# Two-block transformer kernel: block one's expert tokens gathered per expert, with the selection's 32 columns as the stationary operand

## The reference, cut to what matters

```python
def _hier_moe(h, w_rg, b_rg, w_re, b_re, w_gate, w_up, w_down):      # block one
    # h = rms(x) * ffn_norm_g, 256 tokens x 1024
    # best of 4 groups by g_logits; in that group the best 2 of 8 experts
    combine = ...                                   # 256 x 4 x 8, two weights a token, else 0
    for g in range(N_GROUPS):
        a = einsum('td,edf->tef', t, w_gate[g])     # 1024 -> 256
        b = einsum('td,edf->tef', t, w_up[g])
        m = silu(a) * b * combine[:, g, :, None]
        y = y + einsum('tef,efd->td', m, w_down[g]) # 256 -> 1024
```

## Time and profile before

| | |
|---|---|
| median of 3 executions | 914.57 us (913.44 to 915.78) |
| profiled execution | 915.7 us, its span 913.8 us |
| mean granted TensorE clock | 0.992 |
| busy: PE, weight loads, DVE, ACT | 856.8, 552.4, 505.8, 348.6 us |
| DMA moved | 285.35 MB, mean 312 GB/s |
| block one: routing from, first gate/up, last gate/up | 288.6, 312.4, 514.1 us |
| block two: first gate/up, last gate/up | 676.8, 891.3 us |

### The profile page before, as it was taken

The page is one execution under the profiler, slowest core; times in us unless marked ns, Lnnn a source line. Parts: engine busy times, 40 slices in busy tenths (PEclk is TensorE's granted clock), DMA queues, the critical chain, the costliest instruction groups (busy, mean ns, idle before and its releaser), DMA issues.

```text
span 913.8 us, 14985 instructions
## 1 busy us (share of the span) xinstructions
PE 856.8 (94%) x5584; PEld 552.4 (60%) x5584; DVE 505.8 (55%) x1119; ACT 348.6 (38%) x686; POOL 22.3 (2%) x41
## 2 busy tenths in 40 slices
PE   8999999999999998998888899999899999999995
PEld 6778557987977533443333379876664555455552
DVE  5877668555456666433333486789764643333335
ACT  5674435455355322222222366754621111111113
POOL 1010111000000000000000000000000000000000
PEclk9999999999999999999999999999999999999998
DMA  9655894556626899999999997530769899999991
GB/s 356 253 196 223 320 382 190 184 184 232 257 112 258 330 409 362 427 426 425 426 426 425 422 370 294 215 155 1 292 231 369 338 406 423 425 425 425 425 418 55
DMA packets 29958, 285.35 MB, mean 312 GB/s; under 512 B 3113, under 2 KB 5577, under 8 KB 8913
## 3 DMA queue, kind: packets, MB, share of 16 engines
q1 hardware_dynamic: 26400, 278.25, 75.2%
q0 software_dynamic: 1136, 3.74, 1.3%
q10 hardware_dynamic: 2368, 2.64, 0.9%
HBM read 283.56 MB, written 1.06 MB: 311 GB/s over the span
## 4 chain that ended last, share of the span: by engine, by line
PE 65%; DMA 17%; DVE 11%; ACT 4%; issue 2%; SPq 1%; DVEq 0%; ACTq 0%
DMA ring<-in_experts 13%; PE bank L1162 11%; PE bank L743 8%; PE bank L1182 7%; PE bank L745 7%; PE bank L744 7%; PE bank L1210 5%; PE bank L1167 3%; DMA arena<-in_mem 2%; DVE ring_r L526 2%; PE bank L1174 2%; PE bank L1118 2%; DMA ring<-in_ada 1%; PE bank L720 1%; PE bank L1264 1%
## 5 line engine op out<-in xcount | busy, mean ns | idle before, releaser
L526 DVE TENSOR_TENSOR ring_r<-ring,ring_r 128x1024 fp32r<-128x1024 f32 (+1 forms) x84 | 99.4, 1212 | 65.9 <-ACT ring_r L519 65.7
L1162 PE MATMUL bank<-ring,arena 128*64 128x256 f32 x992 | 113.9, 382 | 1.0 <-DVE arena L2498 0.6
L519 ACT ACTIVATE ring_r<-ring 128x1024 fp32r<-128x1024 f32 (+1 forms) x84 | 85.0, 1046 | 68.1 <-PE bank L745 67.4
L743 PE MATMUL bank<-HT_r,ring_r 128*128 128x256 f32 x352 | 102.0, 290 | 1.3 <-DVE arena_r L2066 0.7
L745 PE MATMUL bank<-HT_r,ring_r 128*128 128x256 f32 x352 | 99.6, 283 | 0.0
L1182 PE MATMUL bank<-ring,arena 128*64 128x512 f32 (+1 forms) x488 | 91.7, 604 | 0.7 <-DVE arena L2575 0.7
L1162 PEld LDWEIGHTS bank<-ring,arena 128*64 128x64 f32 x992 | 69.8, 137 | 36.5 <-issue 6.4
L1777 ACT ACTIVATE arena<-bank 128x512 f32<-128x512 f32 (+1 forms) x64 | 31.4, 490 | 137.8 <-PE bank L1162 80.3
L744 PE MATMUL bank<-XN_r,ring_r 128*128 128x256 f32 x288 | 81.5, 283 | 0.0
L1167 PE MATMUL bank<-ring,arena 128*32 128x512 f32 x480 | 57.7, 597 | 22.5 <-DMA ring<-in_experts 22.0
L1210 PE MATMUL bank<-arena_r 64*128 64x512 f32 x496 | 74.1, 417 | 4.3 <-DVE arena_r L2555 3.8
(11 more groups left out here) (503 smaller groups left out, 1422.3 us busy)
## 6 DMA issues: line engine op xcount, KB each, us to landing
ring<-in_experts SPq DMA_DIRECT2D x61, 2048.0 KB, 15.3
ring<-in_experts SPq DMA_DIRECT2D x61, 1024.0 KB, 12.6
ring<-in_ada SPq DMA_DIRECT2D x12, 2048.0 KB, 11.4
ring<-in_win SPq DMA_DIRECT2D x5, 2048.0 KB, 15.1
ring<-in_hy SPq DMA_DIRECT2D x3, 2048.0 KB, 18.1
ring<-in_mk SPq DMA_DIRECT2D x2, 2048.0 KB, 11.0
ring<-in_mv SPq DMA_DIRECT2D x2, 2048.0 KB, 9.5
ring<-in_wo SPq DMA_DIRECT2D x2, 2048.0 KB, 8.7
```

The costliest lines, as they stand in the source:

```text
L519: nc.scalar.activation(R(h), w, ACT.Copy).then_inc(sem("w_high"), 1)
L526: nc.vector.tensor_tensor(R(w), w, R(h), ALU.subtract).then_inc(sem("w_low"), 1)
L743: mm(ps, R(ah), R(bh), start=first, stop=False)
L1162: last = mm(gu_bank[g * wide:(g + 1) * wide, 0:256], xw[:, k, :], w[k // 4][:, k % 4, g * 256:(g + 1) * 256], start=k == 0, stop=k == KD - 1)
```

## The change

The 32 gather matmuls for all 512 positions go. Each expert's window is gathered on its own, in four stages: DVE copies the 32 columns of the selection (`picked`); PE uses them as stationary operand and XN, in fp32, as moving one, for two blocks of tokens and two halves of the channels, each product in a column group of its own (`token_rows`: four matmuls of 512 columns, output 32 pairs x 512 channels each); ACT copies the bank to SBUF (`rows_sb`); PE turns it (`rows_T`: four transposes); DVE adds the two blocks of tokens and scales with the gains into `xwin` (`scaled_tokens`). The split of the tokens in high and low goes in block one, and so do the idle products in the loop. Gather of expert e+2 stands in step e behind `to_tokens`, ahead of down of e-1; the turn of e+1 stands behind `gu_T` of e-1. The first expert's window is compared directly, without the full selection, and what DVE did ahead of the gather for the weights, the ranks and the lists now comes behind the first window.

XN is kept whole for this, so the weights beside the ring move: expert 4's gate/up half to the arena's columns 4096 to 8191, expert 5's to 0 to 4095, its down half to HT. Expert 4's is issued before experts 2 and 3, as soon as the cross attention's last product is done; expert 5's behind expert 3. The bias product of block two moves ahead of the counting products, and POOL loads its operands earlier.

```diff
+        + ([("bias", 1, (5,)), ("cnt1", 1, (0,)), ("cns1", 1, (7,)), ("sct1", 4, (1, 2, 3, 4)), ("slots1", 1, (7,))] if one else
+           [("sct2", 4, (0, 1, 2, 3)), ("cnt2", 1, (6,)), ("cns2", 1, (7,)), ("gx2", 8, (4, 5, 6, 7, 4, 5, 6, 7)), ("slots2", 1, (5,))])
...
+        sorted_at, picked = three(area(at + 3584, TT * (NPAIR + WIN[1])), TT), area(8704, 128).rearrange("p (i t w) -> p i t w", i=2, t=TT)
+        rows_sb = area(8192, 512)
...
-        by_tile = three(area(KD * SORTED + NPAIR, 4096), 4)
-        outside = (((three(XNf[:, :], 4), three(HTf[:, :], 4)), ROW[:, :]),
-                   ((by_tile[:, :, 0:512], by_tile[:, :, 512:1024]), X[:, :, :].rearrange("p t d -> p (t d)")),
+        outside = (((three(area(4096, 2048), 4), three(area(6144, 2048), 4)), ROW[:, :]),
+                   ((three(area(0, 2048), 4), three(area(2048, 2048), 4)), HTf[:, :]),
...
+                for e in range(RING):
+                    if b == 0 and e == 2:
+                        filled(f"xv{XH - 1}")
+                        for q in range(2):
+                            beside_ring(0, q)
+                    in_ring(e)
...
-                    sp.wait_ge(sem("xn_low"), TT)
+                    for q in range(2):
+                        beside_ring(1, q)
                     filled("rt1")
-                    for q in range(2):
-                        beside_ring(0, q)
-                    filled("cns1")
                     sp.dma_start(outside[1][1], w[RING + 1, :, GU:SLOT]).then_inc(sem("outside1"), 16)
-                    for q in range(2):
-                        filled("gx1", 4 * q + 3)
-                        beside_ring(1, q)
...
+                if b == 1:
+                    pe.wait_ge(sem("onehot"), 32)
+                    pe.wait_ge(sem("mask_row"), 1)
+                    ps = take(pe, "bias")
+                    full(mm(ps[0:H1, :], relb[0:BUCKETS + 1, :], oneh[0:BUCKETS + 1, :], start=True, stop=True), "bias")
+                occupy(f"cnt{b}", 0, b)
...
+                def token_rows(i):
+                    for h in range(2):
+                        for t in range(TT):
+                            g = wide * (2 * h + t)
+                            last = mm(list_bank[g:g + wide, :], picked[:, i, t, :], XN[:, t, h * 512:(h + 1) * 512], start=True, stop=True)
+                    return last
+                def rows_T():
+                    for c in range(4):
+                        last = tr(list_bank[:, c * P:(c + 1) * P], rows_sb[:, c * P:(c + 1) * P], ident)
+                    return last
+                def gather_rows(e, i):
+                    pe.wait_ge(sem("picked"), e + 1)
+                    pe.wait_ge(sem("xwin1"), e * 2)
+                    token_rows(i).then_inc(sem("gathered"), 1)
+                def gather_T(e):
+                    pe.wait_ge(sem("rows_sb"), e + 1)
+                    rows_T().then_inc(sem("rows_T"), 1)
...
+                        if b == 1 and not (isinstance(e, int) and e == last_step):
+                            gather_T(e + 1)
+                    first_window = isinstance(e, int) and e == 0
+                    if b == 1:
+                        pe.wait_ge(sem("xwin1"), e * 2 + 2)
+                    elif not first_window:
+                        pe.wait_ge(sem("xwin2"), e)
+                    gate_up(xsT[:, :, 0:wide] if first_window and b == 2 else xwin[:, r % 2], gate_arrived(e, r)).then_inc(sem(f"gu_done{b}"), 1)
+                    if first_window:
                         if b == 1:
-                            for _ in range(1 if isinstance(e, int) and e < unrolled else 3):
-                                mm(list_bank[:, 0:256], ident, T("iota")[:, 0:256], start=True, stop=True)
-                    first_window = isinstance(e, int) and e == 0
-                    if not first_window:
-                        pe.wait_ge(sem(f"xwin{b}"), e)
-                    gate_up(xsT[:, :, 0:wide] if first_window else xwin[:, r % 2], gate_arrived(e, r)).then_inc(sem(f"gu_done{b}"), 1)
-                    if first_window:
+                            gather_rows(1, 1)
+                            gather_T(1)
                         beside_first()
                     if 0 not in first:
                         pe.wait_ge(sem(f"y_low{b}"), e - 1)
                         to_tokens(r % 2).then_inc(sem(f"to_tokens{b}"), 1)
+                    if b == 1 and not (isinstance(e, int) and e + 2 > last_step):
+                        gather_rows(e + 2, r % 2)
                     if isinstance(e, int) and e == last_step:
...
+                if b == 1:
+                    ready(pe, "cnt1")
+                    pe.wait_ge(sem("picked"), 1)
+                    token_rows(0).then_inc(sem("gathered"), 1)
+                    gather_T(0)
+                    ready(pe, "rT1", 1)
...
+            def rows_out(e):
+                act.wait_ge(sem("gathered"), e + 1)
+                A_(rows_sb, expert_banks(1)[3][:, :], ACT.Copy).then_inc(sem("rows_sb"), 1)
...
+                        if e == 0:
+                            rows_out(1)
+                        rows_out(e + 2)
...
+                def scaled_tokens(e, i):
+                    x = expert_tiles(1)[4][:, i]
+                    V.reduce_sum(x, expert_banks(1)[3][:, :].rearrange("p (k t w) -> p k w t", k=KD, t=TT), AXX).then_inc(sem("xwin1"), 1)
+                    dve.wait_ge(sem("xwin1"), e * 2 + 1)
+                    by_half = x.rearrange("p (c h) w -> p c h w", h=2)
+                    gains = C("ffn_norm_g", 0, KD).rearrange("p (h c) -> p c h", h=2)
+                    return V.tensor_tensor(by_half, by_half, gains.unsqueeze(3).broadcast_to([P, 4, 2, WIN[1]]), ALU.mult)
+                def tokens_in(e, i):
+                    dve.wait_ge(sem("rows_T"), e + 1)
+                    if not (isinstance(e, int) and e < 2):
+                        dve.wait_ge(sem("gu_done1"), e - 1)
+                    scaled_tokens(e, i).then_inc(sem("xwin1"), 1)
+                def pick(e, i):
+                    s = window(e, i)
+                    V.tensor_copy(picked[:, i], sorted_at[:, :, bass.ds(s, WIN[1])]).then_inc(sem("picked"), 1)
...
+                    places(picked[:, 0, 0, :], WIN[1], 0)
+                    link(places(picked[:, 0, 1, :], WIN[1], 1))
+                    second_places(picked[:, 0, 0, :], WIN[1], 0)
+                    second_places(picked[:, 0, 1, :], WIN[1], 1).then_inc(sem("picked"), 1)
+                    places(sorted_at[:, 0, 0:NPAIR], NPAIR, 0)
+                    link(places(sorted_at[:, 1, 0:NPAIR], NPAIR, 1))
+                    second_places(sorted_at[:, 0, 0:NPAIR], NPAIR, 0)
+                    second_places(sorted_at[:, 1, 0:NPAIR], NPAIR, 1)
+                    tokens_in(0, 0)
+                    V.memset(sorted_at[:, :, NPAIR:NPAIR + WIN[1]], 0.0).then_inc(sem("pad"), 1)
...
+                if b == 1:
+                    dve.wait_ge(sem("pad"), 2)
+                    pick(1, 1)
                 free(of_tokens(ps), f"cns{b}")
                 ready(dve, f"cns{b}")
                 link(V.reduce_sum(rank4, prod4.rearrange("p k t e -> p (k t) e"), AXX))
+                if b == 1:
+                    weights()
...
+                if b == 1:
+                    tokens_in(1, 1)
+                    pick(2, 0)
+                    pick(3, 1)
...
                 def x_window(e, i):
+                    if b == 1:
+                        tokens_in(e, i)
+                        if not (isinstance(e, int) and e + 2 >= NE):
+                            pick(e + 2, i)
+                        return
                     s = window(e, i)
                     dve.wait_ge(sem(f"gu_done{b}"), e - 1)
```

More of the change, by code:

```diff
@@ L599, in experts, with in_ring @@
                     sp.dma_start(outside[0][1], w[RING, :, GU:SLOT]).then_inc(sem("outside0"), 16)
-                for e in range(RING):
+                first = 3 * RING
+                ways = 2 - b
+                def in_ring(e):
                     load(base + e, w[e, :, 0:GU], GU)
@@ L1141, in beside_first @@
                     full(slot_lists(b, ps), f"slots{b}")
-                    if b == 1:
-                        pe.wait_ge(sem("onehot"), 32)
-                        pe.wait_ge(sem("mask_row"), 1)
-                        ps = take(pe, "bias")
-                        full(mm(ps[0:H1, :], relb[0:BUCKETS + 1, :], oneh[0:BUCKETS + 1, :], start=True, stop=True), "bias")
                 gu_bank, guT_bank, d_bank, list_bank = expert_banks(b)
@@ L1750, in moe @@
                 A_(gex, cand4, ACT.Exp).then_inc(sem("logit_exp"), 1)
-                for k in (0, 1, 2, 3, 4, 6) if b == 1 else range(0, KD, 2):
-                    ps = got(act, f"gx{b}", k)
-                    if shift is None:
-                        last = A_(xsT[:, k, 0:NPAIR], ps[:, :], ACT.Copy, scale=gain(k))
-                    else:
```

(29 more changed lines are left out.)

140 lines of the change are left out of this document (70 added, 70 removed).

## The result

The changed kernel takes 921.31 us (median of 6 runs, 918.88 to 922.94), the one before 914.38 beside it (6 runs, 913.29 to 917.65). The ratio is 1.0063 with a 95% interval of 1.0043 to 1.0082: 5.8 us by the ratio, 6.9 by the medians. Measured a second time it was 923.19 for 914.44, ratio 1.0089 (1.0069 to 1.0108). Forecast were 922.9 and +8.3.

The account below looks back on a forecast made before the run. Bound: bytes moved from 361 us on, so only DMA idle before expert 10's down half counts. Down 6 ends 8.0 us later (0.5, 5.8, 1.8 rounded), plus 0.3 behind it: +8.3, 922.9 us from 914.57; range 917.5 to 926.

Parts of the forecast that it names:

- What sets the time: Block one: expert 6's down product frees the slot for expert 10's down half; DMA idles until that issue, 8.0 us later.
- Earlier loads: Expert 4's gate/up half loaded in the idle stretch before the ring: 4.9 us of transfer moved, worth 0 us.
- The prologue: From the positions to block one's first gate/up product: gather matmuls removed, that product starts at 307.4, 4.9 us earlier.
- The first step takes it back: Gathers and token waits between expert 0's gate/up and down products make down 0 end 0.5 us later.
- Longer steps: Six steps from down 0 to down 6 each gain gather and turn, lose an idle product: +0.97 each, +5.8 us.
- The stalls: Steps 5 to 7: PE waits for DVE's y_low, then for tokens ahead of the gather; 4.9 us together, +1.8.
- Behind it: After expert 10's down half is issued: the next step takes 7.1 us instead of 6.6, adding 0.3 us.
- Rival A: The 4.9 us earlier first gate/up product carries through and added step work is hidden: 909.7 to 913.7 us; chance 0.11.
- Rival B: The gather costs less than its form and DVE pieces vanish in longer steps: about 0, 914.6 us; chance 0.05.
- Rival C: PE's clock falls in prologue without idle products; one or two steps add 6 to 12 us: 929 to 935; chance 0.05.

Follow-up runs that it names:

- b_fill3: Kernel before with three idle products instead of one in each of the first eight expert steps of block one; 916.49 us, ratio 1.0023.
- b_late: Kernel before with DVE's four pieces of the extra windows moved from steps 4 to 7 to steps 25 to 28; 911.01 us, ratio 0.9956.
- a_late: Changed kernel with DVE's four pieces of the extra windows moved to steps 25 to 28; 916.47 us, ratio 1.0021.
- b_late_fill0: Kernel before with DVE's extra-window pieces in steps 25 to 28 and no idle product in the first eight steps; 910.71 us, ratio 0.9956.
- a_loads: Changed kernel with expert 4's gate/up half issued behind expert 3's again, undoing the early load; 923.55 us, ratio 1.0097; on a second occasion 920.98, 1.0077.
- a_again: Changed kernel run once more, unaltered; 923.19 us, ratio 1.0089.
- a_all: Changed kernel with DVE's extra-window pieces in steps 25 to 28, gather behind the down product, idle products in the last step; 916.82 us, ratio 1.0022.
- a_idle: Changed kernel with idle products in its waits: around the first two turns and three in the last expert step; 920.05 us, ratio 1.0059.
- b_last0: Kernel before without the three idle products in block one's last expert step; 916.02 us, ratio 1.0013.
- a_down: Changed kernel with the gather of expert e+2 behind the down product of e-1, ACT's copies reordered to match; 922.97 us, ratio 1.0084.

## Why the prediction was right, and where its sizes were off

- **What sets the time.** Right: the issue of expert 10's down half. b_fill3, b_late and a_late moved it by +2.65, -3.3 and -3.5 us, and block two's first gate/up product went by +2.0, -2.5 and -3.4 (the times by +2.1, -4.0 and -3.8 by the ratios, in which the clock has a part). b_late_fill0 shows the bound of the rule: next to no gain once the engines never idle.
- **Earlier loads, 0.** Right by a_loads: the issue doesn't move.
- **The prologue, 4.9 us earlier.** Right: 4.88 relative. On before's clock the first product starts at 307.48 for the 307.4 forecast.
- **The first step takes it back, +0.5.** Nearly: -0.1. Its chain came nearly as forecast (gate/up 1 at 316.0 on before's clock for 316.35); the down product started 0.86 behind the gather ahead of it, where the forecast had 1.1, and DVE stood idle for 0.31 to 0.33 ahead of most picks, where the forecast had 0.52 for the register load.
- **Longer steps, +5.8.** +5.3: a step grew by 0.88 for 0.97, since a gather takes 0.86 to 0.88 before the next product starts.
- **The stalls, +1.8.** +0.7, the largest miss ahead of the issue. The two waits came in the order forecast, but the second was 1.10 for 1.25, step 5 had 0.32 for 0.6, and the first was 0.51 and 0.76 for 0.75 and 1.0.
- **Behind it, +0.3.** Wrong in sign: -1.2 up to 428 us, of which the faster start of the stream is about 1. Then +1.2 came back by block two, and the clock's fall in the tail, which the sum had at nothing, is 1.5 us by itself. So the sum of +8.3 became +5.9 at block two and +5.8 by the ratio.
- **Where luck helps.** The medians are 6.9 apart, the second time 8.7, and in a_again's profile the issue is 8.2 later than before, close to the forecast 8.0. That closeness isn't the sum's merit: 2.3 of the 8.2 are falls of the clock. The schedule alone gives 5.9 for that 8.0.
- **Rival A, the prologue carries through:** refuted: down 0 ends where it did and the steps are longer. **Rival B, a draw:** refuted; but its half on the DVE pieces was partly true: in b_fill3, where the steps are longer and DVE has no more to do, nearly all of the stalls go.
- **Rival C, the clock:** not what happened, since one fall costs far less than it assumed; but given too low a weight as a cause of smaller losses. It put 6 to 12 us on the prologue. What occurs is a fall of some 4 us at the prologue, in the stalls or in the tail, in some executions and not in others; by the profiles one costs 0.5 to 1.4 us in the prologue (a_late 0.5, a_again 0.7, a_all 1.4), 1.5 and 1.6 in the stalls (a_idle, a_again) and 1.5 in the tail (the change, b_last0). The row used against it (5.38 of 8.00 us busy at 1.00) did not settle it: a_again falls in the prologue behind waits of at most 1.29 us and in the stalls behind 1.10, while a_loads and a_down keep their clock behind 2.77 and 2.76. The Trainium skill (TensorE: Matmul & The Clock Gate, part on the HAM clock gate) has half clock as the default that activity lifts. The traces agree in the direction (a_again's rows), but they don't let one tell which execution falls: in the change's first profile the same waits stand at 1.00 in the same three stretches.

Open: why one execution falls in the prologue, the stalls or the tail and another, of the same kernel with the same waits, does not; and so whether the change costs 5.8 or 8.1 us on a given occasion.

## What to carry to other kernels

Where weights stream at the full rate, look for the last moment at which the DMA engines run dry and for the one instruction whose end issues the next load. Work ahead of it cost here about what it delayed that issue; work behind it cost nothing as long as it fitted beside the transfers, as DVE's four pieces did in steps 25 to 28. A shorter prologue is worth nothing if the steps behind it pay for it. One-off vector work belongs in the steps in which TensorE waits for weights: moving four pieces there gave about 2.5 us in the profile and 3.5 by the medians, more than anything in the change, and b_late (911.01 us) and b_late_fill0 (910.71) are the best versions measured. And before two medians are compared, look at the mean clock of their executions.

## What the runs showed of the hardware

- A wait of 2.75 to 2.96 us on TensorE ahead of the last gate/up product was followed by some 3 to 4 us at the 1.2 GHz level in five profiles of seven, in both kernels (a gate/up product of 2.48 to 3.58 us for 1.92, to_tokens up to 2.07 for 1.20); with idle products ahead of it the wait was 1.44 to 1.55 and none of seven fell. The waits of 1.5 us a step in the loop before it, 375 to 510 us, went by at a clock of 1.00 in all of them.
- The same fall also came behind shorter waits, close together: at most 1.29 us in the prologue and 1.10 in the stalls of a_again. The first profile of the same kernel has the same waits there at 1.00.
- A fall in the tail cost 1.5 us at block two's first gate/up product, in the change and in b_last0, though weights were being transferred at 427 and 428 GB/s (510 to 525 us) all the while.
- Within one kernel, the time of an execution goes with its mean granted clock: the kernel before took 912.5 us at 0.997 and 917.9 at 0.990.
- Two products of the same form behind one another (gather, down) start 0.85 to 0.88 us apart where one alone shows 1.06.
